# Taking 32 of 256 tokens out of a dense expert layer: gathered rows and VectorE sums beside a 224-column up-projection

## Reference

```python
def expert_block(args):
    ht, it, gt = args
    ue = jnp.take(u, it, axis=0)
    act = jax.nn.gelu(jnp.einsum('tkd,td->tk', ue, ht), approximate=False)
    ve = jnp.take(v, it, axis=0)
    return jnp.einsum('tk,tkd->td', gt * act, ve)
```

## Time and profile before

| | us |
|---|---|
| three runs | 1444.06, 1445.22, 1445.54 |
| median | 1445.22 |
| span of the profiled execution, first to last instruction | 1441.8 |

### The profile page before, as it was taken

One profiled execution on the slowest core, in us unless ns is written; L12 is line 12 of the kernel. 1 busy time (PEld: TensorE's weight loads), 2 busy tenths in 40 slices (PEclk: granted clock), 3 DMA queues, 4 the chain that ended last, 5 costly groups with the idle time before them and its releaser, 6 DMA issues.

```text
span 1441.8 us, 25221 instructions
## 1 busy us (share of the span) xinstructions
PE 1422.6 (99%) x10281; PEld 1290.2 (89%) x10281; DVE 967.4 (67%) x1752; ACT 738.5 (51%) x1066; POOL 212.7 (15%) x122
## 2 busy tenths in 40 slices
PE   8999999999999999999999999999999999999997
PEld 7989989999999999998777778888899788899986
DVE  5565674693944777778888876655577864677754
ACT  5674654545454444444444445544567754655543
POOL 5000000488883000000000000000114100000000
PEclk9999999999999999999999999999999999999999
DMA  6433456455555545445545466555543453455552
GB/s 241 142 132 125 138 157 216 141 186 180 187 180 182 170 162 174 164 164 173 174 164 174 164 222 245 181 185 188 175 147 118 159 177 112 154 188 185 181 190 103
DMA packets 67219, 245.07 MB, mean 170 GB/s; under 512 B 7456, under 2 KB 7712, under 8 KB 66848
## 3 DMA queue, kind: packets, MB, share of 16 engines
q1 hardware_dynamic: 66960, 243.19, 50.5%
q10 hardware_dynamic: 144, 0.26, 0.0%
HBM read 242.37 MB, written 1.05 MB: 169 GB/s over the span
## 4 chain that ended last, share of the span: by engine, by line
PE 77%; issue 14%; DVE 4%; ACT 4%; POOL 1%; DMA 0%; POOLq 0%; SPq 0%; DVEq 0%; ACTq 0%
PE bank L433 76%; ACT A L1154 2%; DVE wlo L1712 1%; ACT whi L1154 1%; PE bank L442 1%; DVE A L1712 1%; ACT L1154 1%; DVE A L1708 0%; DVE xres L1712 0%; DMA xres<-in_x 0%; POOL wlo L2555 0%; ACT hTh L1154 0%; DVE small L2361 0%; DVE small L1712 0%; POOL small L2561 0%
## 5 line engine op out<-in xcount | busy, mean ns | idle before, releaser
L1712 DVE TENSOR_TENSOR wlo<-raw,whi 128x1024 fp32r<-128x1024 f32 (+1 forms) x375 | 458.1, 1223 | 334.3 <-ACT whi L1154 333.9
L1154 ACT ACTIVATE whi<-raw 128x1024 fp32r<-128x1024 f32 (+1 forms) x450 | 472.9, 1053 | 401.3 <-PE bank L433 401.3
L433 PE MATMUL bank<-hTh,whi 128*128 128x256 f32 x1944 | 555.5, 286 | 2.0 <-DVE wlo L1712 1.3
L433 PE MATMUL bank<-hTl,whi 128*128 128x256 f32 x1944 | 548.6, 282 | 0.0
L433 PE MATMUL bank<-hTh,wlo 128*128 128x256 f32 x1944 | 548.0, 282 | 0.0
L433 PEld LDWEIGHTS bank<-hTh,whi 128*128 128x128 f32 x1944 | 367.0, 189 | 5.9 <-DVE wlo L1712 2.1
L433 PEld LDWEIGHTS bank<-hTh,wlo 128*128 128x128 f32 x1944 | 366.0, 188 | 0.0
L433 PEld LDWEIGHTS bank<-hTl,whi 128*128 128x128 f32 x1944 | 365.5, 188 | 0.3 <-issue 0.2
L433 PE MATMUL bank<-whi,hTh 128*128 128x512 f32 (+2 forms) x552 | 218.4, 396 | 0.2
L433 PE MATMUL bank<-wlo,hTh 128*128 128x512 f32 (+2 forms) x552 | 215.0, 390 | 0.0
L433 PE MATMUL bank<-whi,hTl 128*128 128x512 f32 (+2 forms) x552 | 214.9, 389 | 0.0
(11 more groups left out here) (178 smaller groups left out, 1391.8 us busy)
## 6 DMA issues: line engine op xcount, KB each, us to landing
raw<-in_u SPq DMA_DIRECT2D x128, 512.0 KB, 3.3
raw<-in_v SPq DMA_DIRECT2D x128, 512.0 KB, 3.3
raw<-in_w_up SPq DMA_DIRECT2D x44, 512.0 KB, 3.3
raw<-in_w_down SPq DMA_DIRECT2D x22, 512.0 KB, 3.2
raw<-in_w_in_t SPq DMA_DIRECT2D x17, 512.0 KB, 3.4
raw<-in_w_in_g SPq DMA_DIRECT2D x16, 512.0 KB, 3.3
raw<-in_w_out SPq DMA_DIRECT2D x16, 512.0 KB, 4.0
raw<-in_w_pq SPq DMA_DIRECT2D x16, 512.0 KB, 3.5
```

The lines of the kernel that those rows point to most:

```text
L433: return e.matmul(o, l, r, start=st, stop=sp_, skip_group_check=True)
L1154: return e.activation(o, i, func, **kw)
L1712: return e.tensor_tensor(o, a, b, op)
```

## The change

Tokens 0 to 31 leave the dense layer. Their 32 x 128 picked rows are laid out as 32 picks for each of 128 partitions (four partitions to a token). GpSimd fetches them: 32 indirect DMAs of 128 rows of `u` (512 KB each) at every second unit from unit 44 of the up stage on, and 32 of `v` at every second unit from unit 56 of the down stage on. VectorE multiplies each gathered tile of `u` with `hrep`, the normalised token, and sums along the row in one instruction of 128 x 1024 (`pick_u`, every second unit from 48 to 110); ScalarE takes Gelu of the 32 columns; VectorE adds gate x Gelu x row of `v` up in `pk_acc` (`pick_v`, every second unit from 60 to 122). Two float32 matmuls with a 0/1 matrix add `pk_acc` to the down stage's sums. The dense up-projection runs on 224 columns, `gates` has 2 x 28 groups and starts at unit 70 rather than 62, and `acts` is packed at 224 columns. GpSimd's share of the `wlo` changes: units 0 to 43 as before, then only every second one from 44 to 61 and from 72 to 111 (in place of 44 to 61 entirely and none behind).

```diff
 def on_pool(i):
 
     slot = i - 2
-    if BASE["u"] <= slot < BASE["u"] + 62:
+    z = slot - BASE["u"]
+    if 0 <= z < GATHER_AT or (GATHER_AT <= z < 62 or 72 <= z < DOT_AT + 2 * NPK) and z % 2:
         return True
```

```diff
-                            ins = three(banks[bk][:, (n % 2) * 256:(n % 2 + 1) * 256], [z[:, j, k, :] for z in wv],
-                                        [z[:, k, :] for z in src], k == 0, k == K - 1)
+                            ins = three(banks[bk][:, (n % 2) * 256:(n % 2 + 1) * 256 - c0], [z[:, j, k, :] for z in wv],
+                                        [z[:, k, c0:T] for z in src], k == 0, k == K - 1)
...
-            lin_T(BASE["u"], 62, hTv, KD, steps=U1_STEPS)
+            lin_T(BASE["u"], 62, hTv, KD, steps=U1_STEPS, c0=NG)
             side.drain()
+            lin_T(BASE["u"] + 62, G_DENSE - 62, hTv, KD, c0=NG)
             side.lists[0] += [gates(0), gates(1)]
-            lin_T(BASE["u"] + 62, 66, hTv, KD)
+            lin_T(BASE["u"] + G_DENSE, P - G_DENSE, hTv, KD, c0=NG)
...
+                if m == 127:
+                    e.wait_ge(s["pk_used"], 2 * NPK)
+                    for h in range(2):
+                        mm(banks[h][0:NG, :], K_("pick"), pk_acc[:, h * 512:(h + 1) * 512], False, False)
```

```diff
+            def rep_h(j):
+                q = slice(NG * j, NG * j + NG)
+                if j == 0:
+                    e.wait_ge(s_gffn, 16)
+                    e.wait_ge(s["r_add"], 4)
+                    e.wait_ge(s["n_rstd"], 3)
+                own(stt(hrep[q, :], xres[0:NG, 0:D], small[0:NG, 2:3], hrep[q, :], ALU.mult, ALU.mult))
+
+            def pick_u(u):
+                if REP_AT <= u < REP_AT + 2 * NJ and (u - REP_AT) % 2 == 0:
+                    rep_h((u - REP_AT) // 2)
+                g, r = divmod(u - DOT_AT, 2)
+                if r == 0 and 0 <= g < NPK:
+                    if g == 0:
+                        again()
+                    e.wait_ge(*pk_landed(g))
+                    z = pk_buf(g)
+                    stt(z, z, 1.0, hrep, ALU.mult, ALU.mult, accum_out=pk_dot[:, g:g + 1]).then_inc(s["pk_used"], 1)
+
+            def pick_v(n):
+                if n == ACC_V - 2:
+                    e.wait_ge(s["pk_act"], 1)
+                    own(tt(pk_co, pk_co, pk_gate, ALU.mult))
+                i, r = divmod(n - ACC_V, 2)
+                if r == 0 and 0 <= i < NPK:
+                    e.wait_ge(*pk_landed(NPK + i))
+                    again()
+                    z, c = pk_buf(NPK + i), pk_co[:, i:i + 1]
...
+                        e.wait_ge(s["pk_used"], NPK + i)
+                        ins = stt(pk_acc, z, c, pk_acc, ALU.mult, ALU.add)
+                    ins.then_inc(s["pk_used"], 1)
```

```diff
+            def gather(g):
+                if g == 0:
+                    e.wait_ge(s["pk_idx"], 1)
+                if g == EARLY:
+                    e.wait_ge(s["rt_dve"], 8)
+                if g >= 3 and not EARLY <= g < EARLY + 3:
+                    e.wait_ge(s["pk_used"], g - 2)
+                table, i = (utab, g) if g < NPK else (vtab, g - NPK)
+                e.indirect_dma_start(out=pk_buf(g), out_offset=None, in_=table,
+                                     in_offset=bass.IndirectOffsetOnAxis(ap=pk_idx[:, i:i + 1], axis=0)
+                                     ).then_inc(s_pick[pk_slot(g)], 16)
```

More of the change, by code:

```diff
@@ L33 @@
 GATE_UP = 2.0 ** 15
+NG = 32
+NJ = P // NG
+NPK = P // NJ
+TD = T - NG
+NGRP = TD // OB
+EARLY = 12
+G_DENSE = 70
+REP_AT, GATHER_AT, DOT_AT = 38, 44, 48
+GATHER_V, ACC_V = 56, 60
+MEM_AT = 81
 STREAMS = [
@@ L241, in build @@
         s_raw = [sem(f"s_raw{i}") for i in range(NRAW)]
+        s_pick = [sem(f"s_pick{i}") for i in range(6)]
+        s_gffn = sem("s_gffn")
         s_in, s_in2, s_keep, s_con0, s_con1, s_con2, s_keys, s_w2c, s_gf, s_gf2, s_mem, s_out, s_w0, s_rest = (
@@ L557, in normed, with lin_T @@
                 return lambda k: e.wait_ge(s["n_lo"], 8 * j + 2 * (k // 2) + 2) if k % 2 == 0 else None
-            def lin_T(u0, units, src, K, first=None, after=None, steps=(1,)):
+            def lin_T(u0, units, src, K, first=None, after=None, steps=(1,), c0=0):
                 per = KD // K
@@ L777, in gates @@
                 o2 = og[:, :].rearrange("p (m j i r) -> p m j i r", m=OP, j=2, r=2)
-                for g in range(T // OB):
-                    G = 32 * half + g
+                for g in range(NGRP):
+                    G = NGRP * half + g
                     bk = gate_bank(half, g)
@@ L2105, in cut_acts @@
                 e.wait_ge(s["ca_hi"], n + 1)
-                tt(cut(1, n), acts[:, n, :], cut(0, n).bitcast(F32), ALU.subtract).then_inc(s["ca_lo"], 1)
+                if n == 2:
+                    for z in (hTh, hTl):
+                        own(e.memset(t3(z[:, :].bitcast(F32), 8)[:, :, 0:NG], 0.0))
+                    again()
+                tt(cut(1, n)[:, NG:T], acts[:, n, :], cut(0, n)[:, NG:T].bitcast(F32), ALU.subtract
+                   ).then_inc(s["ca_lo"], 1)
             def mem_norm():
@@ L2452, in dve_program @@
             side.lists[0] += [routing(0), routing(1)]
-            lin_T(BASE["u"], 62, steps=U1_STEPS)
+            lin_T(BASE["u"], 62, before=pick_u, steps=U1_STEPS)
             side.drain()
+            lin_T(BASE["u"] + 62, G_DENSE - 62, before=lambda u: pick_u(u + 62))
             side.lists[0] += [gates(0), gates(1)]
-            lin_T(BASE["u"] + 62, 66)
+            lin_T(BASE["u"] + G_DENSE, P - G_DENSE, before=lambda u: pick_u(u + G_DENSE))
+            for z in first_cut:
+                own(e.memset(t3(z[:, :].bitcast(F32), 2)[:, :, 0:NG], 0.0))
+            again()
             cut_acts(0)
             cut_acts(1)
+            e.wait_ge(s["w"], BASE["v"])
             for n in range(128):
@@ L2565, in units @@
                     lo(i + 2)
+                    g, r = divmod(i - BASE["u"] - GATHER_AT, 2)
+                    if r == 0 and 0 <= g < NPK:
+                        gather(g)
                     side.step(steps[(i + 1) % len(steps)])
@@ L2614, in pool_program @@
                     continue
+                i, r = divmod(n - GATHER_V, 2)
+                if r == 0 and 0 <= i < NPK:
+                    gather(NPK + i)
                 side.step()
-                if n == 72:
+                if n == MEM_AT:
                     side.lists[0].append(mem_norm())
```

76 lines of the change are left out of this document (54 added, 22 removed).

## The result

The kernel takes 1461.99 us after the change (median of four runs, 1460.59 to 1465.0) and 1445.11 us before: a ratio of 1.0123, 95% interval 1.0108 to 1.0137. It is 16.9 us slower, where 5.9 were forecast. The direction was right and the time lies in the range, but the loss is nearly three times the one forecast. The profiled execution of after is its slowest, 1465.0 us with a span of 1463.2; its mean granted clock is 0.987, that of the other three 0.988 to 0.990, so TensorE's clock was low for longer in it than in the median execution.

A forecast was written before the change was run, and what follows sets the result against it. TensorE, busy 99% of the span, was taken as the bound. The terms -25.2 - 4.6 + 1.7 + 8.0 + 26 gave +5.9 us, 1451.1 us on the median, with a range of 1422 to 1469.

The forecast's parts named there:

- 224 columns: Up stage, 3072 matmuls cut from 256 to 224 columns: 8.2 ns less each, -25.2 us.
- The floor: TensorE matmul price at few columns: flat at 0.1118 us, so 224 columns stand on it.
- the straight line: Rival on TensorE: time falls straight from 256 to 128 columns, gain only 6.3 us, sum 1470; 8%.
- the column rule: Rival on TensorE: gap is columns / 2.4 + 2.5 ns, cut worth 41 us, 1435 with the stalls; 2%.
- the corner: TensorE matmul price: sloped line meets the floor 18 columns below 256, at 238.
- Eight groups fewer: Gate groups on TensorE: 64 become 56 at 0.58 us each, -4.6 us.
- Two float32 matmuls: End of TensorE's stream: two added matmuls cost +1.7 us.
- What was hidden: Gathers, DMA share of 0.87, down stage and small steps: covered by other work, 0 us.
- Units 48 to 56: Up stage: TensorE waits for VectorE's `wlo` amid dots, routing chunks and holds by GpSimd, +8 us.
- the walk: Step-by-step count of VectorE's work from the end of unit 43: stalls 3.3, 4.4 and 0.3 us, sum 8.0.
- Units 72 to 111: Up stage: GpSimd's `wlo` holds VectorE; TensorE stands 2.6 us every second pair, +26 us over 20 pairs.
- The rival without exclusion: VectorE and GpSimd don't exclude each other at this length: 72 to 111 costs 0 to 5 us, total 1425; 36%.

The follow-up runs named there:

- e5_pad: The kernel before with 32 unused columns of zeros at the end of the constants tile, nothing else changed: 1434.4 us against 1443.78, ratio 0.9929.
- e1_dense: The changed kernel without gathers, products, weighted sums and the two float32 matmuls, `wlo` split as before the change: 1408.03 us against 1445.12, ratio 0.9748.
- e2_gather: The changed kernel with all 64 gathers and its own `wlo` split, without VectorE's products, sums and copies and the two matmuls: 1413.6 us, ratio 0.978.
- e6_late: The changed kernel with u's gathers and products begun 14 units later, GpSimd making all `wlo` to unit 61, none behind: 1421.8 us, ratio 0.9846.
- e3_nopool72: The changed kernel with VectorE instead of GpSimd making GpSimd's 20 `wlo` of units 72 to 111: 1433.46 us, ratio 0.9921.
- e4_warm: The changed kernel with matmuls on zeros ahead of the `og` wait in every second group of units 72 to 111: 1456.52 us, ratio 1.0084.

## Why the prediction was right or wrong

**The ledger.** Forecast, and measured by medians:

| step | forecast | measured | between |
|---|---|---|---|
| place of the tiles | 0 | -9.4 | before, e5_pad |
| 224 columns and eight groups fewer | -29.8 | -26.4 | e5_pad, e1_dense |
| everything that is added | +35.7 | +54.0 | e1_dense, after |
| sum | +5.9 | +18.2 | (16.9 directly; the lines come from different sets of runs) |

The third line can be split by loads of the up stage, whose first and last start mark the stage. In after, then in e1_dense, the `raw` loads of `u` (ns minimum, median and maximum, then first and last start): 414.5 us and 363.5.

```profile
L2764 SPq DMA_DIRECT2D raw<-in_u x128: 327/328/432, 244.5 to 659.0; - x128
```

```profile
L2754 SPq DMA_DIRECT2D raw<-in_u x128: 327/328/328, 243.3 to 606.8; - x128
```

The difference, 51.0 of the 57.0 us between the two profiled spans, is 24.7 of waits for `og`, 13.8 - 4.0 = 9.8 more of waits for `wlo`, 13.6 of slow clock, and 2.9 beside these. Of the 2.9 some 1.6 stand around the stalls: two pairs with a stall and no slow stretch take 14.51 us, where 2 x 5.93 + 2.49 = 14.35, ten times; 1.3 I can't place. Outside the stage lie 1.2 us ahead of it, which is the slow stretch near 165 us that e1_dense's execution lacks, 1.2 in the down stage, and 3.6 behind: 1.9 for the two matmuls and 1.6 at the very end. From the last issue of an output transfer to the end of the span it is 4.7 us in after and in every kernel with gathers, e2_gather too, and 3.1 in every one without; why the end of the program takes longer with them isn't shown.

**224 columns: right in the rule, and the term was mis-sized.** The floor is there: 24 matmuls in 2.68 us, which is what was forecast, and neither the straight line's 0.118 each nor the 0.096 of the column rule of the Trainium skill (TensorE: Matmul & The Clock Gate, section Back-to-back issue gap). What was wrong is the side that I took for firm. The 0.1200 of the earlier trace rows isn't the price of 256 columns but that of 256 columns in this place; where after has its tiles it is 0.1184. On that the cut is worth 3072 x 7.1 ns = 21.8 us, not 25.2. With 0.2333 for 512 columns the slope is 0.449 ns a column, and the corner lies 7.1/0.449 = 16 columns below 256, at 240. The 1.6 ns of each 256-column matmul, and 0.9 ns of each with 512, came as a gain of their own. The sum of both is 36 us where 29.8 stood, so that in the end this step erred to the good side.

**Eight groups fewer: -4.6, about right.** An untouched pair takes 5.93 us, where 5.95 was forecast; less its two units that is 5.93 - 2 x 2.68 = 0.57 a group, 4.6 for eight. It is also what is left of the 26.4 (26.4 - 21.8).

**Two float32 matmuls: right, 1.9 for 1.7.** After, order of time, TensorE, at the end of the down stage: 2.70 us from the matmul ahead of them to the second one behind. The same three starts in e1_dense, without them, lie at 995.36, 995.81 and 996.12, 0.76 us, so they cost 1.9.

```profile
1048.72 0.39 PE L462 MATMUL bank<-whi,hTl 128*128 128x512 f32 x1
1049.29 1.88 PE L462 MATMUL bank<-A,keep 128*32 128x512 f32 x4 [0.18 <-issue]
...
1051.42 0.39 PE L462 MATMUL bank<-wlo,hTh 128*128 128x512 f32 x1
```

**What was hidden stayed hidden.** The DMA share reached the forecast 0.87 from 450 to 480 us and was 0.80 over 180 us of e2_gather, the issue is 0.96 us on GpSimd, e2_gather bounds both at 5.6 us, and the down stage lost 376.1 - 374.9 = 1.2 us. Raw loads landed after 3.7 us in place of 3.3, mostly within their cover: ScalarE waited 2.0 us for them once in after, and 3.2 in e6_late. What the forecast left out, and not only put at 0, are the 1.6 us at the end of the program.

**Units 48 to 56: 8 forecast, 9.8 measured, in another place.** The stalls of 2.07, 2.07 and 5.69 us add up to about the forecast, but by the starts of TensorE's units they stand ahead of units 46, 48 and 54, where the walk has them ahead of 52, 54 and 56. (The units of the walk and of `on_pool` count VectorE's steps, and the `wlo` made at a step is that of the unit two further on; so the stalls belong to steps 44, 46 and 52, not 50, 52 and 54.) I had let VectorE begin the stage in step at the end of unit 43; the copies of `h` (1.29 us at 385.95) and a chunk of eight `MAX8` (2.71 at 387.28) had made it late before. Chunks plus held operations on a VectorE that had been ahead is what e6_late takes away, and the loss goes with it; that size and total agree while the places don't is in part luck.

**Units 72 to 111: the waits right, nearly to the number.** 26 us forecast by a walk through two pairs, 24.7 measured, and pairs of 7.7 us on average (138.6 us for 18 of them) where 7.2 were forecast, the slow clock being in them; the walk said that `og_eq` is held, that TensorE then stands 2.6 us, and that every second pair keeps up, and the rows show 2.49, in every second pair. The rival without exclusion is refuted by the row of 2.58 us (the rule of the Trainium skill, SBUF — State Buffer, section Who interferes with whom, agrees: VectorE's instruction has two inputs in SBUF, and GpSimd's reads SBUF), and e3_nopool72 shows the cause by taking it away. The product with two inputs in SBUF was the right row to size the hold by, and not the short operations of the earlier trace rows.

**The step that failed: stalls were priced at their length alone.** The prediction's sum adds stalls to a stream whose pace it takes as fixed at a clock of 1.00, since that is what the earlier trace rows show. Before has no stall in these stretches, so no row of it could show what follows one. After a stall of 2.5 us the clock was 0.50 for 3.4 us in six cases of ten, and each cost 1.6 us more. Two stalls of the stage ahead of them met a low clock too, one of them for longer. This is the largest miss, 13.6 us by the trace of after, where the sum has nothing; e4_warm takes all six stretches of units 72 to 111 away by keeping TensorE busy and is 5.5 us faster in the medians, though its fillers cost something. With +13.6 for the clock, +1.8 and -1.3 for the two stall terms, +0.2 for the two matmuls, and -9.4 and +3.4 on the dense side the sum is +14.2. These sizes come from profiled executions, and their spans differ by 1463.2 - 1441.8 = 21.4. The 7.2 that lack are the 2.9 beside the waits, 1.2 for the slow stretch near 165 us, 1.2 in the down stage and 1.6 at the end; 0.3 is left. The medians differ by 4.5 less than the spans. For 3.0 of this the profiled execution of after is its slowest, and that of before lies 1.5 below its median (a run lasts 1.8 us longer than its span); by the granted clocks (0.987 against 0.988 to 0.990) the clock's share in a median execution is, as an estimate, some 3 us below 13.6. The gain from the place hid two thirds of the clock's loss; measured against the padded kernel the change costs 1462.0 - 1434.4 = 27.6 us.

## What to carry to other kernels

Before work is split between VectorE and GpSimd, look whether VectorE's steps with two inputs in SBUF will meet GpSimd steps that read SBUF: here VectorE's 0.42 us step took 2.58 beside a GpSimd step, and doing 20 of GpSimd's steps on the busier VectorE won 28.5 us. Price a stall of TensorE at its length plus the slow stretch that can follow, here 1.6 us after six of ten stalls of about 2.5. When a change moves allocations, run the old kernel with the same shift before crediting or blaming the change: here it was 9.4 us of 1445, as much as many a change is worth.

## What the runs showed of the hardware that was not expected

The pace of matmuls with 256 moving columns depended on where the tiles lie: 24 in 2.88 us at the old place and 64 columns (256 bytes a partition) behind it, 2.84 at 32 columns, 2.85 at 8 columns. With 224 columns at the place of 32 they took 2.68. Which tile and which boundary count is open. A VectorE step that met a GpSimd `wlo` ended behind that one's end by its own length less about 0.15 us (0.27 for an `og_eq` of 0.42, 1.08 for a dot of 1.22). The slow clock was granted for 3.4 us after some stalls of 2.5 us and not after others of the same length; what tells these apart isn't shown either. The read of the product's sum (the `DVE_READ_ACCUMULATOR` row) takes 0.08 us, so that the whole dot is 1.2 us.
